# Feed-forward up products with rounded rows and their remainders side by side behind one load of rounded weights

## The reference

```
D_MODEL = 1024
SEQ = 256
DEPTH = 2
D_FF = 2816
...
def causal_dwconv(u, w, b):
    s = u.shape[1]
    up = jnp.pad(u, ((0, 0), (CONV_W - 1, 0), (0, 0)))
    y = b
    for j in range(CONV_W):
        y = y + up[:, j:j + s, :] * w[j]
    return y
...
        x = x + jnp.concatenate([o_fox, o_diff, o_mla], axis=-1) @ w_o[i]
        up = causal_dwconv(rmsnorm(x, ln2_g[i]) @ w_up[i], conv_w[i], conv_b[i])
        g, u = up[..., :D_FF], up[..., D_FF:]
        x = x + (jax.nn.silu(g) * u) @ w_down[i]
```

## Time and profile before

| | us |
|---|---|
| median of 3 runs | 1913.53 (1911.83 to 1913.66) |
| the profiled execution | 1913.8 |
| its span, first to last instruction | 1911.9 |
| TensorE busy | 1530.2 (80%) |
| VectorE busy | 790.9 (41%) |
| ScalarE busy | 572.6 (30%) |
| granted TensorE clock, mean | 0.907 of full speed |

### The profile page before, as it was taken

How to read it: one execution, slowest core, us unless ns; L and a number is a source line. 1 busy time by engine, 2 the same in 40 slices (tenths; PEclk the granted TensorE clock), 3 DMA queues, 4 the chain that set the end, 5 groups by cost and what they waited for, 6 DMA issues and landing times.

```text
span 1911.9 us, 26314 instructions
## 1 busy us (share of the span) xinstructions
PE 1530.2 (80%) x11284; PEld 1158.5 (61%) x11284; DVE 790.9 (41%) x1237; ACT 572.6 (30%) x906; POOL 62.6 (3%) x56
## 2 busy tenths in 40 slices
PE   8999999999999999997635556479999663555646
PEld 8999999899999899982201212139998220121212
DVE  4557777656777798740100101019864010010101
ACT  4455555445555475320000000017532000000001
POOL 1010000101000000100000000002010000000000
PEclk9999999999999999998877878789999887787868
DMA  9307556431755294599999999997459999999997
GB/s 299 127 30 246 195 178 189 125 111 59 265 178 178 88 302 134 199 361 421 427 427 427 427 428 427 428 389 240 143 189 382 420 427 427 427 427 427 427 427 306
DMA packets 174186, 560.85 MB, mean 293 GB/s; under 512 B 12208, under 2 KB 134502, under 8 KB 146294
## 3 DMA queue, kind: packets, MB, share of 16 engines
q1 hardware_dynamic: 165558, 551.49, 74.2%
q10 hardware_dynamic: 8512, 7.68, 1.3%
HBM read 558.09 MB, written 1.05 MB: 292 GB/s over the span
## 4 chain that ended last, share of the span: by engine, by line
PE 56%; issue 22%; DMA 15%; DVE 3%; ACT 1%; SPq 1%; POOL 0%; POOLq 0%; PEldq 0%; ACTq 0%; DVEq 0%
PE psum L2576 8%; PE psum L2546 5%; PE psum L2828 5%; PE psum L2523 4%; PE psum L2525 4%; PE psum L2524 4%; DMA ring<-in_w_gate 3%; DMA ring<-in_w_down 3%; DMA ring<-in_w_up 3%; PE psum L2692 2%; DMA arena<-in_w_down 2%; PE psum L2810 2%; PE psum L2441 2%; PE psum L2643 2%; DMA arena<-in_w_up 2%
## 5 line engine op out<-in xcount | busy, mean ns | idle before, releaser
L2828 PE MATMUL psum<-ring,arena 128*32 128x512 f32 (+1 forms) x1600 | 279.7, 691 | 182.9 <-DMA ring<-in_w_down 76.1
L2828 PE MATMUL psum<-arena 128*32 128x512 f32 x1024 | 207.8, 707 | 141.3 <-DMA ring<-in_w_up 41.8
L2828 PEld LDWEIGHTS psum<-ring,arena 128*32 128x32 f32 x1600 | 69.9, 128 | 331.0 <-issue 328.0
L915 DVE TENSOR_TENSOR W<-ring,W 128x2048 fp32r<-128x2048 f32 (+1 forms) x96 | 213.9, 2228 | 124.1 <-ACT W L910 123.7
L910 ACT ACTIVATE W<-ring 128x2048 fp32r<-128x2048 f32 (+1 forms) x96 | 178.5, 1860 | 84.5 <-PE psum L2525 40.0
L2523 PE MATMUL psum<-XT,W 128*128 128x256 f32 x704 | 200.1, 284 | 0.2
L2525 PE MATMUL psum<-XT,W 128*128 128x256 f32 x704 | 199.1, 283 | 0.0
L2524 PE MATMUL psum<-XT,W 128*128 128x256 f32 x704 | 199.1, 283 | 0.0
L2828 PEld LDWEIGHTS psum<-arena 128*32 128x32 f32 x1024 | 50.0, 127 | 244.3 <-issue 244.1
L2166 DVE TENSOR_TENSOR arena<-arena,psum 128x512 f32<-128x512 f32 x16 | 11.0, 688 | 432.9 <-PE psum L2828 432.9
L2576 PE MATMUL psum<-rounded_slot,rounded_slot 128*128 128x256 f32 x1216 | 177.8, 285 | 0.6 <-DVE rounded_slot L815 0.6
(11 more groups left out here) (331 smaller groups left out, 2689.3 us busy)
## 6 DMA issues: line engine op xcount, KB each, us to landing
ring<-in_w_down SPq DMA_DIRECT2D x36, 2048.0 KB, 29.5
ring<-in_w_up SPq DMA_DIRECT2D x32, 2048.0 KB, 29.0
ring<-in_w_up SPq DMA_DIRECT2D x58, 1024.0 KB, 5.2
ring<-in_w_in SPq DMA_DIRECT2D x56, 1024.0 KB, 7.1
ring<-in_w_gate SPq DMA_DIRECT2D x28, 2048.0 KB, 34.0
arena<-in_w_up SPq DMA_DIRECT2D x24, 2048.0 KB, 31.5
arena<-in_w_down SPq DMA_DIRECT2D x20, 2048.0 KB, 29.7
arena<-in_w_gate SPq DMA_DIRECT2D x20, 2048.0 KB, 29.7
```

What stands on the lines that cost most here:

```text
L915: nc.vector.tensor_tensor(W2[split_pair(v)][:, c], slot(v % SLOTS_1)[:, c], W1[split_pair(v)][:, c].bitcast(F32), ALU.subtract).then_inc(r ...
L2828: last = nc.tensor.matmul(psum[CAP * e:CAP * (e + 1), b, 0:cols.stop - cols.start], src[:, 4 * half + k, CAP * e:CAP * (e + 1)], tiles[e][ ...
```

## The change

It touches up(0) to up(9) of both layers; up(10) keeps its three matmuls.

- `XT1` and `XT2` become two halves of one buffer, `XT_BOTH`. One matmul of 512 columns multiplies `w1` by both; a second one of 256 columns multiplies `w2` by `XT1` and adds to the first half. A step has 64 matmuls instead of 96, and as many columns.
- The results need a whole bank for each g and m: bank 4 + 2g + m, columns 0 to 255 `w1*XT1 + w2*XT1`, columns 256 to 511 `w1*XT2`. All four banks are used in each step, so up(j) waits, for each g, until VectorE has read the banks of step j - 1.
- ScalarE copies the second halves of both banks into `up_second` (one instruction for each g). VectorE adds the first halves to it (`up_whole`), and then multiplies by the norms, in ordinary memory. The last taps and the eight earlier taps read `up_whole` instead of PSUM.
- The reciprocal norms are turned in bank 3 instead of bank 6, and down(0) waits for their copy.

```diff
+                        if j < FF_STEPS - 1:
+                            if j:
+                                act.wait_ge(up_scaled, past(up_scaled) + 4 * (j - 1) + 2 * g + 1)
+                            nc.scalar.activation(up_second[:, g], psum[:, 4 + 2 * g:6 + 2 * g, S:2 * S], ACT.Copy).then_inc(tap2, 1)
+                        act.wait_ge(up_scaled, past(up_scaled) + (4 * j + 2 * g + 2 if j < FF_STEPS - 1 else 4 * j + g + 1))
                         for m in range(2):
                             c = g * FF_CH + 2 * j + m
                             last = nc.scalar.activation(
-                                y[:, j % 2, g, m, :], psum[:, 4 + 2 * (j % 2) + g, m * S:(m + 1) * S], ACT.Identity,
+                                y[:, j % 2, g, m, :], up_whole[:, g, m], ACT.Identity,
...
                     for g in range(2):
                         dve.wait_ge(up_mm, past(up_mm) + 2 * j + g + 1)
-                        both = psum[:, 4 + 2 * (j % 2) + g, :].rearrange("p (m s) -> p m s", m=2)
-                        nc.vector.tensor_tensor(both, both, roots.unsqueeze(1).broadcast_to([P, 2, S]), ALU.mult).then_inc(up_scaled, 1)
+                        first = psum[:, 4 + 2 * g:6 + 2 * g, 0:S]
+                        both_roots = roots.unsqueeze(1).broadcast_to([P, 2, S])
+                        if j < FF_STEPS - 1:
+                            dve.wait_ge(tap2, past(tap2) + 4 * j + 2 * g + 1)
+                            nc.vector.tensor_tensor(up_whole[:, g], first, up_second[:, g], ALU.add).then_inc(up_scaled, 1)
+                            dve.wait_ge(up_scaled, past(up_scaled) + 4 * j + 2 * g + 1)
+                            nc.vector.tensor_tensor(up_whole[:, g], up_whole[:, g], both_roots, ALU.mult).then_inc(up_scaled, 1)
+                        else:
+                            nc.vector.tensor_tensor(up_whole[:, g], first, both_roots, ALU.mult).then_inc(up_scaled, 1)
...
-                                    out=dst, in0=psum[:, 4 + 2 * (j % 2) + g, m * S:m * S + S - tap],
+                                    out=dst, in0=up_whole[:, g, m, 0:S - tap],
...
                 def up(j):
-                    if j >= 2:
-                        pe.wait_ge(conv, past(conv) + 2 * (j - 1))
-                    if j == 1:
-                        pe.wait_ge(root_table, past(root_table) + 2)
                     for g in range(2):
+                        if j:
+                            pe.wait_ge(up_scaled, past(up_scaled) + 4 * (j - 1) + 2 * g + 1)
...
-                                nc.tensor.matmul(dst, w1[:, k, c], XT1[:, k, :], start=(k == 0), stop=False)
-                                nc.tensor.matmul(dst, w1[:, k, c], XT2[:, k, :], start=False, stop=False)
-                                last = nc.tensor.matmul(dst, w2[:, k, c], XT1[:, k, :], start=False, stop=(k == KD - 1))
+                                if j < FF_STEPS - 1:
+                                    nc.tensor.matmul(psum[:, bank, :], w1[:, k, c], XT_BOTH[:, :, k, :], start=(k == 0), stop=False)
+                                else:
+                                    nc.tensor.matmul(psum[:, bank, 0:S], w1[:, k, c], XT1[:, k, :], start=(k == 0), stop=False)
+                                    nc.tensor.matmul(psum[:, bank, 0:S], w1[:, k, c], XT2[:, k, :], start=False, stop=False)
+                                last = nc.tensor.matmul(psum[:, bank, 0:S], w2[:, k, c], XT1[:, k, :], start=False, stop=(k == KD - 1))
```

More of the change, by code:

```diff
@@ L278 @@
     "root_rows_then_table": (2, 3, 0),
-    "up_products_scaled": (22, 0, 0), "turned_in_psum": (13, 13, 0), "turned_first_parts_by_dve": (4, 0, 0), "turned_first_parts_by_act": (12, 1, 0),
+    "up_products_summed_then_scaled": (42, 0, 0), "turned_in_psum": (13, 13, 0), "turned_first_parts_by_dve": (4, 0, 0), "turned_first_parts_by_act": (12, 1, 0),
     "turned_second_parts": (19, 5, 0), "weights_first_parts": (49, 24, 0), "weights_second_parts": (49, 24, 0),
@@ L291 @@
     "diff_normalised": (1, 0, 0), "output_projected": (4, 4, 0), "residual_after_mixer": (4, 4, 0),
-    "up_projected": (22, 0, 0), "last_tap": (22, 0, 0), "middle_tap": (11, 0, 0), "convolved": (22, 0, 0),
+    "up_projected": (22, 0, 0), "second_rows_copied_and_last_tap": (42, 0, 0), "middle_tap": (11, 0, 0), "convolved": (22, 0, 0),
     "gates_silu": (11, 0, 0), "hidden_ready": (12, 0, 0), "down_projected": (14, 0, 0),
@@ L344, in build @@
         W2 = [split_buffer("W2_0", 2, [P, SLOT_W]), split_buffer("W2_1", 3, [P, SLOT_W]), in_place_of("W2_2", XT, 0, [P, SLOT_W])]
-        XT1, XT2 = (split_buffer(f"XT{i + 1}", 4 + i, [P, KD, S]) for i in range(2))
+        XT_BOTH = split_buffer("XT_both", 4, [P, 2, KD, S])
+        XT1, XT2 = XT_BOTH[:, 0], XT_BOTH[:, 1]
         where1, table1 = first_constants()
@@ L427, in build @@
         dsqs = mqr.rearrange("p h s -> p (h s)").rearrange("p (u n) -> p u n", n=DIFF_V)
+        up_second = place(2 * 2 * S).rearrange("p (g m s) -> p g m s", g=2, m=2)
+        up_whole = place(2 * 2 * S).rearrange("p (g m s) -> p g m s", g=2, m=2)
         end_att = cursor[0]
@@ L599, in build @@
         root_table = sem("root_rows_then_table")
-        up_scaled = sem("up_products_scaled")
-        tap2 = sem("last_tap")
+        up_scaled = sem("up_products_summed_then_scaled")
+        tap2 = sem("second_rows_copied_and_last_tap")
         tap1 = sem("middle_tap")
@@ L1789, in _ @@
                 dve.wait_ge(turned, past(turned) + 4 * 3 + 1)
-                nc.vector.tensor_copy(roots, psum[:, 6, 0:S]).then_inc(root_table, 1)
+                nc.vector.tensor_copy(roots, psum[:, 3, 0:S]).then_inc(root_table, 1)
                 dve.wait_ge(root_table, past(root_table) + 2)
@@ L1797, in _ @@
                         dve.wait_ge(up_mm, past(up_mm) + 2 * j + g + 1)
-                        both = psum[:, 4 + 2 * (j % 2) + g, :].rearrange("p (m s) -> p m s", m=2)
-                        nc.vector.tensor_tensor(both, both, roots.unsqueeze(1).broadcast_to([P, 2, S]), ALU.mult).then_inc(up_scaled, 1)
+                        first = psum[:, 4 + 2 * g:6 + 2 * g, 0:S]
[7 more added lines that the diff above has]
+                            nc.vector.tensor_tensor(up_whole[:, g], first, both_roots, ALU.mult).then_inc(up_scaled, 1)
                         if FF_OF[j, g] + W_BUFS < USES_1:
                             split_rest(dve, past, FF_OF[j, g] + W_BUFS)
-                    dve.wait_ge(tap2, past(tap2) + 2 * (j + 1))
+                    dve.wait_ge(tap2, past(tap2) + (4 * (j + 1) if j < FF_STEPS - 1 else 4 * j + 2))
                     for tap, col, done in ((1, C_W1, tap1), (2, C_W0, conv)):
@@ L2514, in up @@
                             for t in range(TT):
-                                last = nc.tensor.transpose(psum[:, 6, t * P:(t + 1) * P], token_roots[:, t, :], ident)
+                                last = nc.tensor.transpose(psum[:, 3, t * P:(t + 1) * P], token_roots[:, t, :], ident)
                             last.then_inc(turned, 1)
@@ L2518, in up @@
                         for m in range(2):
-                            dst, c = psum[:, 4 + 2 * (j % 2) + g, m * S:(m + 1) * S], slice(m * P, (m + 1) * P)
+                            bank, c = 4 + 2 * g + m, slice(m * P, (m + 1) * P)
                             for k in range(KD):
@@ L2522, in up @@
                                     pe.wait_ge(xt_rest, past(xt_rest) + KD + 3 + k + 1)
-                                nc.tensor.matmul(dst, w1[:, k, c], XT1[:, k, :], start=(k == 0), stop=False)
-                                nc.tensor.matmul(dst, w1[:, k, c], XT2[:, k, :], start=False, stop=False)
-                                last = nc.tensor.matmul(dst, w2[:, k, c], XT1[:, k, :], start=False, stop=(k == KD - 1))
+                                if j < FF_STEPS - 1:
[4 more added lines that the diff above has]
+                                last = nc.tensor.matmul(psum[:, bank, 0:S], w2[:, k, c], XT1[:, k, :], start=False, stop=(k == KD - 1))
                         last.then_inc(up_mm, 1)
                 def down(j):
+                    if j == 0:
+                        pe.wait_ge(root_table, past(root_table) + 2)
                     w1, w2 = (t.rearrange("p (k n) -> p k n", k=2) for t in split_ready(FF_OF[j, 2]))
```

1 line of the change is left out of this document (removed).

## The result

The changed kernel takes 1941.85 us (median of 4 runs, 1938.54 to 1944.51), the kernel before in the same measurements 1912.68 us: 1.53% slower, ratio 1.0153, 95% interval 1.0139 to 1.0166. Forecast were 1938.9 us, in a range of 1924 to 1951. The profiled execution took 1941.0 us with a span of 1939.2, 27.3 longer than before.

The account below looks back on a forecast made before the run. TensorE set the pace at 17.01 us; additions of 2.61 would lengthen the VectorE-ScalarE chain from 15.32 to 17.93, making it the bound. 12.7 us a layer, 25.4 in all, on 1913.5 gave 1938.9 us, range 1924 to 1951.

Parts of the forecast that it names:

- 1.70 of slack in the chain: VectorE-ScalarE work takes 15.32 us a step by itself; ScalarE's rounding waits 1.70 us for TensorE's g = 1 products.
- 0.07: ScalarE's two last taps of g = 0 read memory instead of PSUM: 0.07 us more a step.
- 0.50: ScalarE's copy for g = 1, behind the weight rounding, adds 0.50 us a step.
- 0.60: VectorE's product with the norms for g = 1, no longer hidden by ScalarE's rounding, adds 0.60 us a step.
- TensorE's part: Pairing matmuls in up saves TensorE 0.35 us a step, giving 16.66 us; at most 7.0 us in all.
- 0.72: VectorE's sum of first and second halves, once for g = 0 and once for g = 1: 0.72 us each.
- +2.8: Start of a layer: down(1) comes at 193.95 instead of 191.1, 2.8 us later.
- +7.4: Middle of a layer: the intervals from down(1) to down(9) cost 8 x 0.92 us, 7.4 in all.
- +2.5: End of a layer: down(10) comes 9.4 us behind down(9) instead of 6.9, 2.5 more.
- rival 4: Clock falls to 1.2 GHz behind the long wait, so down(10) takes twice its 5.5 us: 1950 us; chance 0.09.
- Rival 1: VectorE's taps and products get cheaper reading memory, 0.65 us off the chain: 1926 us; chance 0.12.
- Rival 2: Chain stays under TensorE's 16.66 us a step, so the saving arrives: 1906.5 us; chance 0.06.

Follow-up runs that it names:

- The order changed in the kernel before: Kernel before the change, with only ScalarE's rounding of the down weights moved ahead of silu: 1912.92 us, ratio 1.0003.
- the control: Kernel with the copy and the down weights' rounding moved forward, but three matmuls of 256 columns again: 1912.89 us, ratio 1.0000 to the kernel before.
- kernel with 14 small products: Changed kernel with 14 small unused products into bank 4 in TensorE's wait before down(10) of each layer: 1938.51 us, ratio 1.0137.

## Why the prediction was right

**What bounds the kernel.** TensorE's 17.01 us with 1.70 of slack in the chain. Copy without sum confirms it: by the prediction's terms its chain is 15.32 + 0.07 + 0.50 + 0.60 = 16.49, and it measured 16.51, with no loss. The order changed in the kernel before fits too (no gain).

**TensorE's part.** 16.66 us a step and 7.0 us in all were forecast. Without copy and sum it was 6.8 us by the medians (6.2 by the two stretches), and the control gave 6.5 to 7.1. The size of a spared matmul was 0.011 by rows of `down`; the steps without a wait average 16.69 (below).

**The chain.** The terms were 0.72, 0.07, 0.50, 0.72 and 0.60, the sum 17.93. Measured: 17.93. From start to start in the rows above they are 0.72, 0.06, 0.54, 0.73 and 0.61; the eight taps add 0.03, and the last taps for g = 0 start 0.73 behind the product and not 0.79, 0.06 less. So the terms are right to some 0.05, and that the second decimal of the sum agrees is luck. The sums are 1.42 of it by experiment, against 1.44; the copy taken twice gives 0.48 for one more. ScalarE's last taps take 595 ns out of memory, 39 more than out of PSUM, against the 35 assumed. That the copy for g = 0 is hidden holds as well: the sum for g = 0 follows the hidden remainder by 0.60 with no wait.

**The layer put together.** +2.8, +7.4 and +2.5 were forecast, down(9) 10.2 later and down(10) 12.7. Measured in the first layer: +2.6 (down(1) at 193.73 against 191.09), +7.6 (0.3 of it the one step of 18.21) and +2.5; together 10.3 and 12.8. The first two misses cancel in part.

**What was left out.** Two terms. The clock was rival 4, held apart with 0.09 and priced at 5.5 us a layer for the whole of down(10); it came on top of the forecast and not in its place, for a part of the first half only: 1.6 us. A clock under 1.00 in the feed-forward stretches was one of the prediction's own signs of being wrong, and it came (0.83); it touched the size, not the chain. And the squared gain in the second layer, 1.1 us, wasn't in the sum at all; it stands on VectorE, in the time that had been slack. A sum for a chain that is about to lose its slack has to go through everything on its engines, and not through one typical step. With both, two layers are 25.5 + 3.2 + 1.1 = 29.8, of which the second block's -2.4 took some in the profiled execution. The medians differ by 29.2, the forecast had 25.4.

**The rivals.** Rival 1, memory operands that are cheaper for VectorE, was wrong: the taps take 478 ns out of memory against 475 out of PSUM, a 128x512 tensor_tensor 692 with both inputs in memory against 688 with one in PSUM. The table of the Trainium skill (VectorE: DVE Perf Modes, The TRN2 errata — SBUF-src ops pay a fixed extra latency per instruction), by which the fixed part is 58 cycles for a memory source and 120 for one in PSUM, isn't borne out for these forms of two tensors. Rival 2, that the chain has room, is not what this kernel does, but it names the right place: it said that the gain would arrive if the copy, the sum and the product for g = 1 lay beside the weight rounding, and with the copy moved there a part of it did (1910.2 us), with the rounding of the down weights moved too all of it (1906.4).

## What to carry to other kernels

A full engine says what the pace is, and not how much room the others have: follow one period through the engines that hand work to each other, take out the one link that waits for the full engine, and compare that length with the period. Additions to that chain are free up to the slack and cost in full beyond it (apart from the first and last periods), and an operation of 0.6 us in front of or behind another one in an in-order queue can decide which it is. When a saving on the full engine brings nothing, look for the order that hides the new work before giving the saving up.

## What the runs showed of the hardware

The step of TensorE with pairs is not one number. In the kernel without copy and sum, where nothing is waited for, the `down` of successive steps start 16.61 and 16.78 us apart in turn (190.70, 207.31, 224.09, 240.70, 257.49 us), where the kernel before has 17.01 each time. With 5.50 us for the `down`, a pair of 512 and 256 columns takes 0.347 us in the shorter steps and 0.353 in the longer ones. Both hold the same matmuls. It is not simply odd against even steps: in the second layer of the kernel with the copy and the down weights moved forward every step takes 16.79 us (515.94, 532.72, 549.51, 566.30 us). What makes the difference stays open.

The clock fell behind a wait of 2.7 us as well: down(1) of the changed kernel took 7.1 us to the next matmul instead of 5.5, and the stretch around it was granted 0.86. TensorE's idle time took it up: down(2) still started 0.4 us late (212.10 us, where 0.75 behind the hidden remainder is 211.67), but the hidden remainders stayed 17.93 us apart, and down(3) started at its place.

The length of the wait alone doesn't say what the clock will do. In the kernel with 14 small products, the same as the changed one up to there, it stayed at 1.00 behind a wait of 2.55 us before down(1) of the first layer (first row below is the changed kernel, the second this one), and it fell behind one of 2.01 us in the second layer (third row). In the kernel with the copy but without the sum the waits before down(10) are 1.98 and 1.97 us; its first half took 2.86 us in the first layer and 4.41 in the second, where the clock had fallen.

```profile
192.00:204.00 12.00, 10.27 (x43) 8.46 (x44) 10.58 (x13) 5.50 (x8) 0.00 (x0) 0.86 0.53 176
192.00:204.00 12.00, 10.22 (x51) 8.63 (x52) 10.58 (x13) 5.54 (x8) 0.00 (x0) 1.00 0.57 184
590.00:600.00 10.00, 9.38 (x37) 7.68 (x38) 8.62 (x10) 4.47 (x6) 0.00 (x0) 0.83 0.63 211
```
